# One of the conditioning's chunks is summed under ga and oa, and the first down projection makes a low part more in front of each four additions

## What is computed

```python
mod = (silu(c) @ ada_w + ada_b)          # ada_w is 1024 x 6144
shift_m, scale_m, gate_m, shift_f, scale_f, gate_f = split(mod, 6)
h = rmsnorm(x, pre_norm_mix) * (1 + scale_m) + shift_m
...                                       # h @ w_in, attention, state space mixer
x = x + gate_m * rmsnorm(mix, post_norm_mix)
h2 = rmsnorm(x, pre_norm_ffn) * (1 + scale_f) + shift_f
x = x + gate_f * rmsnorm(swiglu(h2), post_norm_ffn)
```

## Time and the profile before

| | us |
|---|---|
| median of 3 runs | 1008.52 (1007.31 to 1011.36) |
| the profiled execution's own time | 1003.94 |
| its span, from the first instruction to the last | 1002.2 |
| PE busy | 947.4 (95%) |
| DVE busy | 666.9 (67%) |
| ACT busy | 544.0 (54%) |
| POOL busy | 292.9 (29%) |

### The profile page before, as it was taken

One profiled execution on the slowest core, in us unless ns is written; L12 is line 12 of the kernel. 1 busy time (PEld: TensorE's weight loads), 2 busy tenths in 40 slices (PEclk: granted clock), 3 DMA queues, 4 the chain that ended last, 5 costly groups with the idle time before them and its releaser, 6 DMA issues.

```text
span 1002.2 us, 16492 instructions
## 1 busy us (share of the span) xinstructions
PE 947.4 (95%) x6119; PEld 831.1 (83%) x6119; DVE 666.9 (67%) x1067; ACT 544.0 (54%) x956; POOL 292.9 (29%) x260
## 2 busy tenths in 40 slices
PE   7999998999989989889999999989989989999997
PEld 6987777888877788789989999988879878888786
DVE  4765656777787568975567656677966577755553
ACT  5567565444433666834456456557863664444443
POOL 4304114111123455689951034330230241000010
PEclk9999999999999999999999999999999999999999
DMA  9755336789989713562028566652226667665562
GB/s 258 224 168 156 120 117 207 237 272 284 283 276 334 221 58 96 157 169 74 22 64 286 176 168 185 172 148 85 85 86 227 218 194 226 217 217 170 191 219 74
DMA packets 141467, 179.03 MB, mean 179 GB/s; under 512 B 8010, under 2 KB 117260, under 8 KB 141392
## 3 DMA queue, kind: packets, MB, share of 16 engines
q1 hardware_dynamic: 130624, 144.53, 46.4%
q0 software_dynamic: 10176, 33.16, 11.3%
q10 hardware_dynamic: 592, 0.34, 0.1%
HBM read 176.89 MB, written 1.12 MB: 178 GB/s over the span
## 4 chain that ended last, share of the span: by engine, by line
PE 80%; DVE 8%; ACT 5%; DMA 3%; issue 2%; POOL 1%; ACTq 0%; DVEq 0%; SPq 0%
PE bank L1923 26%; PE bank L2012 12%; PE bank L2014 12%; PE bank L2013 12%; DVE w_lo L1334 2%; ACT w_hi L873 1%; PE bank L2050 1%; PE bank L2181 1%; DVE isc L1727 1%; PE bank L1954 1%; PE bank L2460 1%; PE bank L2440 1%; PE bank L2436 1%; PE bank L2375 1%; PE bank L2547 1%
## 5 line engine op out<-in xcount | busy, mean ns | idle before, releaser
L1334 DVE TENSOR_TENSOR w_lo<-w_raw,w_hi 128x1024 fp32r<-128x1024 f32 (+1 forms) x227 | 274.7, 1236 | 94.3 <-ACT w_hi L873 88.0
L873 ACT ACTIVATE w_hi<-w_raw 128x1024 fp32r<-128x1024 f32 (+1 forms) x258 | 261.8, 1036 | 131.0 <-PE bank L2014 53.9
L1923 PE MATMUL bank<-h_hi,w_hi 128*128 128x256 f32 x560 | 163.4, 292 | 6.2 <-POOL w_lo L705 2.1
L1923 PE MATMUL bank<-h_lo,w_hi 128*128 128x256 f32 x560 | 158.3, 283 | 0.0
L1923 PE MATMUL bank<-h_hi,w_lo 128*128 128x256 f32 x560 | 158.2, 282 | 0.0
L2012 PE MATMUL bank<-w_hi,h_hi 128*128 128x512 f32 x384 | 152.3, 397 | 1.9 <-DVE h_lo L1334 1.9
L2014 PE MATMUL bank<-w_hi,h_lo 128*128 128x512 f32 x384 | 150.2, 391 | 0.0
L2013 PE MATMUL bank<-w_lo,h_hi 128*128 128x512 f32 x384 | 150.1, 391 | 0.0
L705 POOL TENSOR_TENSOR w_lo<-w_raw,w_hi 128x1024 fp32r<-128x1024 f32 (+1 forms) x39 | 86.4, 2215 | 149.6 <-DVE w_lo L1334 112.3
L1923 PEld LDWEIGHTS bank<-h_hi,w_hi 128*128 128x128 f32 x560 | 107.2, 191 | 7.8 <-POOL w_lo L705 2.3
L1923 PEld LDWEIGHTS bank<-h_lo,w_hi 128*128 128x128 f32 x560 | 107.3, 192 | 0.0
(11 more groups left out here) (458 smaller groups left out, 1850.8 us busy)
## 6 DMA issues: line engine op xcount, KB each, us to landing
w_raw<-in_w_in SPq DMA_DIRECT2D x84, 512.0 KB, 3.8
ada_raw<-in_ada_w POOLq DMA_DIRECT2D x48, 512.0 KB, 6.0
w_raw<-in_w_gate_up SPq DMA_DIRECT2D x88, 256.0 KB, 5.3
w_raw<-in_w_ffn_in SPq DMA_DIRECT2D x88, 256.0 KB, 3.8
w_raw<-in_w_down SPq DMA_DIRECT2D x22, 512.0 KB, 6.7
w_raw<-in_w_ffn_out SPq DMA_DIRECT2D x22, 512.0 KB, 4.4
w_raw<-in_w_out SPq DMA_DIRECT2D x16, 512.0 KB, 4.2
w_raw<-in_w_o_ssd SPq DMA_DIRECT2D x16, 512.0 KB, 3.5
```

The costliest lines, as they stand in the source:

```text
L873: act.activation(high(u, n), w_raw[:, u % RING, 0:n], ACT.Copy).then_inc(hi_ready, 1)
L1334: return dve.tensor_tensor(dst, src, hi.bitcast(F32), ALU.subtract)
L1923: ins = pe.matmul(out_b[:, s, :], w[:, kk, c], x[:, k0 + k, :], start=k == 0 and s == 0 and step == 0, stop=k == sum(st.ks) - 1 and s == 1 ...
```

## The change

`MOD_CHUNKS` gives the columns a new order: the chunk counters 0 to 6 stand for the chunks 0, 1, 2, 3, 6, 7 and 4 (shift_m, scale_m, shift_f and half of gate_m), the counters 7 to 9 for chunks 8, 9 and 5 (scale_f and the other half of gate_m). Counters 0 to 6 are summed up to the first down projection, counters 7 to 9 under ga and oa, three steps in each block instead of two. Under the first down projection there are four turns instead of six, and each `split_to` reaches one unit further, so that in the first turn one low part stands in front of the additions, and the pairs of the later turns end one unit further on.

`store_sums` and `finish_mod` follow the new order: the first store is three DMAs instead of two, the second two instead of one, the first load of `mod` two instead of one. The second `finish_mod` loads rows 0 to 39, works on all 48 rows, and stores rows 16 to 23 and 32 to 39. `mod` is set to zero once at the start.

```diff
@@ -519,6 +519,8 @@
     n_rows_dma = 9
+    MOD_CHUNKS = (0, 1, 2, 3, 6, 7, 4, 8, 9, 5, 10, 11)
+    MOD_FIRST, MOD_SECOND = 7, 10
@@ -729,36 +731,49 @@
             pool.dma_start(ada_raw[:, j, :].rearrange("p (k c) -> p k c", k=2),
-                           ada[:, 2 * j:2 * j + 2, 512 * c:512 * c + 512]).then_inc(ada_in[j], 16)
+                           ada[:, 2 * j:2 * j + 2, 512 * MOD_CHUNKS[c]:512 * MOD_CHUNKS[c] + 512]).then_inc(ada_in[j], 16)
         def store_sums(part):
             pool.wait_ge(sums_read, part + 1)
             if part == 0:
-                for g in range(2):
-                    pool.dma_start(sums_dram[2 * D * g:2 * D * (g + 1)].rearrange("(j n) -> j n", j=4),
-                                   sums[0:P:32, g, :]).then_inc(sums_out, 16)
+                pool.dma_start(sums_dram[0:2 * D].rearrange("(j n) -> j n", j=4), sums[0:P:32, 0, :]).then_inc(sums_out, 16)
+                pool.dma_start(sums_dram[3 * D:4 * D].rearrange("(j n) -> j n", j=2), sums[0:64:32, 1, :]
+                               ).then_inc(sums_out, 16)
+                pool.dma_start(sums_dram[2 * D:2 * D + 512].rearrange("(j n) -> j n", j=1), sums[64:65, 1, :]
+                               ).then_inc(sums_out, 16)
+            elif part == 1:
+                pool.dma_start(sums_dram[4 * D:5 * D].rearrange("(j n) -> j n", j=2), sums2[0:64:32, 0, :]
+                               ).then_inc(sums_out, 16)
+                pool.dma_start(sums_dram[2 * D + 512:3 * D].rearrange("(j n) -> j n", j=1), sums2[64:65, 0, :]
+                               ).then_inc(sums_out, 16)
...
-            pool.wait_ge(sums_out, (32, 48, 64)[part])
+            pool.wait_ge(sums_out, (48, 80, 96)[part])
+        mod_parts = (((0, 20), (24, 32)), ((0, 40),), ((32, 48),))
+        mod_stores = (((0, 32),), ((16, 24), (32, 40)), ((32, 48),))
         def finish_mod(n, r0, r1):
+            for a0, a1 in mod_parts[n]:
+                pool.dma_start(mod[a0:a1, :], sums_dram[P * a0:P * a1].rearrange("(r n) -> r n", n=P)).then_inc(sums_in, 16)
+            pool.wait_ge(sums_in, 16 * (5 + sum(len(p) for p in mod_parts[:n + 1])))
             at_rows = slice(r0, r1)
-            pool.dma_start(mod[at_rows, :], sums_dram[P * r0:P * r1].rearrange("(r n) -> r n", n=P)).then_inc(sums_in, 16)
-            pool.wait_ge(sums_in, 16 * (n + 6))
...
-            pool.dma_start(mod_dram[P * r0:P * r1].rearrange("(r n) -> r n", n=P), mod[at_rows, :]).then_inc(mod_out, 16)
-            pool.wait_ge(mod_out, 16 * (n + 1))
+            for a0, a1 in mod_stores[n]:
+                pool.dma_start(mod_dram[P * a0:P * a1].rearrange("(r n) -> r n", n=P), mod[a0:a1, :]).then_inc(mod_out, 16)
+            pool.wait_ge(mod_out, 16 * sum(len(p) for p in mod_stores[:n + 1]))
...
+        pool.memset(mod[:, :], 0.0)
         link(pool.memset(mod_g[:, :], 1.0))
@@ -771,10 +786,9 @@
-        for h in range(16):
-            if h < 14:
-                for j in (0, 1) if h % 2 == 0 else (2, 3):
-                    load_ada(h // 2 + 1, j)
+        for h in range(2 * (MOD_FIRST - 1)):
+            for j in (0, 1) if h % 2 == 0 else (2, 3):
+                load_ada(h // 2 + 1, j)
@@ -813,17 +827,16 @@
         pool.wait_ge(uv_mm, 4)
-        for j in range(4):
-            load_ada(8, j)
-        for j in range(4):
-            load_ada(9, j)
+        for c in range(MOD_FIRST, MOD_SECOND):
+            for j in range(4):
+                load_ada(c, j)
...
-        finish_mod(1, 32, 40)
+        finish_mod(1, 0, 48)
@@ -1256,7 +1269,7 @@
-        act.activation(sums2[0:64, 0, :], bank[6][0:64, :], ACT.Copy).then_inc(sums_read, 1)
+        act.activation(sums2[0:96, 0, :], bank[6][0:96, :], ACT.Copy).then_inc(sums_read, 1)
@@ -1656,8 +1669,8 @@
         gate_up(0, s_gu)
-        for h in range(6):
-            split_to(s_dn.u0 + AHEAD + 2 * h)
+        for h in range(2 * (MOD_FIRST - 5)):
+            split_to(s_dn.u0 + AHEAD + 2 * h + 1)
             modulate(5 + h // 2, 4 * (h % 2), 4 * (h % 2) + 4)
         boundary(1, 0)
@@ -1787,10 +1800,12 @@
         for b in range(s_ga.n):
             split_to(s_ga.u0 + 2 * b + 2 + AHEAD)
-            modulate(8, 2 * b, 2 * b + 2)
+            for step in range(3 * b, 3 * b + 3):
+                modulate(MOD_FIRST + step // KD, step % KD, step % KD + 1)
         for b in range(s_oa.n):
             split_to(s_oa.u0 + 2 * b + 2 + AHEAD)
-            modulate(9, 2 * b, 2 * b + 2)
+            for step in range(3 * (s_ga.n + b), 3 * (s_ga.n + b) + 3):
+                modulate(MOD_FIRST + step // KD, step % KD, step % KD + 1)
@@ -2357,7 +2372,7 @@
-                between={(0, 0): last, (1, 0): lambda: add_up(0, 8, 0), (1, 5): shift_transpose})
+                between={(0, 0): last, (1, 0): lambda: add_up(0, MOD_FIRST, 0), (1, 5): shift_transpose})
@@ -2482,7 +2497,7 @@
-        add_up(8, 10, 6)
+        add_up(MOD_FIRST, MOD_SECOND, 6)
```

More of the change, by code:

```diff
@@ L737, in store_sums @@
             if part == 0:
-                for g in range(2):
-                    pool.dma_start(sums_dram[2 * D * g:2 * D * (g + 1)].rearrange("(j n) -> j n", j=4),
-                                   sums[0:P:32, g, :]).then_inc(sums_out, 16)
-            else:
-                pool.dma_start(sums_dram[D * (3 + part):D * (4 + part)].rearrange("(j n) -> j n", j=2),
-                               (sums2 if part == 1 else sums)[0:64:32, 0, :]).then_inc(sums_out, 16)
-            pool.wait_ge(sums_out, (32, 48, 64)[part])
+                pool.dma_start(sums_dram[0:2 * D].rearrange("(j n) -> j n", j=4), sums[0:P:32, 0, :]).then_inc(sums_out, 16)
[8 more added lines that the diff above has]
+                               ).then_inc(sums_out, 16)
+            else:
+                pool.dma_start(sums_dram[5 * D:6 * D].rearrange("(j n) -> j n", j=2), sums[0:64:32, 0, :]
+                               ).then_inc(sums_out, 16)
+            pool.wait_ge(sums_out, (48, 80, 96)[part])
+        mod_parts = (((0, 20), (24, 32)), ((0, 40),), ((32, 48),))
+        mod_stores = (((0, 32),), ((16, 24), (32, 40)), ((32, 48),))
         def finish_mod(n, r0, r1):
+            for a0, a1 in mod_parts[n]:
+                pool.dma_start(mod[a0:a1, :], sums_dram[P * a0:P * a1].rearrange("(r n) -> r n", n=P)).then_inc(sums_in, 16)
+            pool.wait_ge(sums_in, 16 * (5 + sum(len(p) for p in mod_parts[:n + 1])))
             at_rows = slice(r0, r1)
-            pool.dma_start(mod[at_rows, :], sums_dram[P * r0:P * r1].rearrange("(r n) -> r n", n=P)).then_inc(sums_in, 16)
-            pool.wait_ge(sums_in, 16 * (n + 6))
             link(pool.tensor_tensor(mod[at_rows, :], mod[at_rows, :], mod_b[at_rows, :], ALU.add))
@@ L867, in split @@
             if s_lat.u0 <= u < s_lat.u0 + 4:
-                act.wait_ge(sums_out, 32)
+                act.wait_ge(sums_out, 48)
             elif u in held:
@@ L1281, in _ @@
         act.wait_ge(cum_ready, 1)
-        act.wait_ge(sums_out, 48)
+        act.wait_ge(sums_out, 80)
         for i in range(KI + 4):
```

## The result

| | before | after |
|---|---|---|
| median of 5 runs, us | 1008.52 (1006.44 to 1011.36) | 1001.87 (1000.19 to 1003.07) |
| ratio | | 0.9929 [0.9904, 0.9955] |
| the profiled execution's own time, us | 1003.94 | 1003.07 |
| its span, us | 1002.2 | 1001.4 |
| its mean granted clock of TensorE | 0.994 | 0.994 |

The median is 6.3 us under the forecast and 2.1 us under the range. The two profiled executions tell another story: they differ by 0.8 us of span (forecast: 0.3). So the first thing to settle is why the medians of the two kernels lie 6.7 us apart while their profiles hardly differ.

A forecast was written before the change was run, and what follows sets the result against it. TensorE, busy 95% of the span, was taken as the bound. The sum was 1002.2 - 1.4 (head) + 1.1 (handoff) = 1001.9 us of span, so the median goes from 1008.52 to 1008.2 us, range 1004.0 to 1012.3.

The forecast's parts named there:

- the last of the sum: From span to median: the profiled execution's 4.6 us under the median carries over, so the median goes from 1008.52 to 1008.2.
- The low part in front of the additions: Start of first down projection: unit 2 gains 2.8 us, unit 3 newly stalls about 1.4 us, net gain 1.4 us.
- faster landings or a freer DVE give nothing there: First down projection: removing eight additions and four 512 KB loads gains nothing, PE having no gap after 294.5.
- The lead holds at units 5, 7 and 9: First down projection: low parts of these units are ready in time, with margins of 0.2, 0.4 and 0.5 us.
- The head's term: Start of the first down projection: net gain of 1.4 us, bounded by 0 and 2.8.
- nobody waits for them: POOL's nine small loads behind `gu_T` start up to 10 us sooner, at no cost.
- rival 4: First down projection: the stall only moves on to unit 3 and units 5, 7, 9; head gain 0, median 1009.6; chance 0.14.
- The handoff: Sums and `mod` through DRAM before the transpose: extra store and load pieces add 1.1 us, all paid by PE.
- Rival 2: Handoff through DRAM: pieces serialize, plus 5.0 us instead of 1.1, median 1012.1; chance 0.09 with its half-way case.
- Rival 1: Handoff through DRAM: less traffic makes the chain 0.4 us shorter instead of 1.1 longer, median 1006.7; chance 0.14.
- Under ga and oa, the second store, the rest: Later blocks and POOL's later work: extra additions, loads and DMAs cost 0, with a DMA share of 0.92.
- Rival 3: Under ga and oa: DMA runs short, a weight unit lands late, plus 5.5 us, median 1013.7; chance 0.03.

The follow-up runs named there:

- five later comparisons: The changed kernel, no edit, timed again five times against the kernel before: ratios 0.9992, 0.9982, 0.9978, 0.9977 and 0.9971.
- the chunks alone: The changed kernel with the old `split_to`, so one chunk less is summed early but low parts stand as before: ratio 1.0017 against the kernel before.
- the pieces alone: The kernel before with its first store of sums in three DMAs and its first load of `mod` in two: ratio 0.9987.
- the low parts alone: The kernel before with each `split_to` under the first down projection reaching one unit further, all eight chunks kept there: ratio 1.0010.

## Why the prediction was wrong

**The step that failed is the last of the sum:** "The profiled execution lies 4.6 us under the median of the three runs shown; a difference carries over", with "a median of the new kernel may stand about 3 us to either side of its case". The 4.6 us are no fixed offset between a profiled execution and a median. They are the spread of single executions, and this spread goes with the granted clock. Against that kernel's mean of 1006.73 us at 0.9872, the median stood 1.8 us above and the profiled execution 2.8 us below; it had 0.994, for which the fit gives 0.0068 x 590 us = 4.0 us below. All five executions of the new kernel in the first comparison had 0.994 or 0.995, mean 0.9944, so its median came out near the profiled execution and not above it. The 6.65 us between the medians then go like this, by the fit: 0.6 us the program, 0.0072 x 590 = 4.2 us the clock of the five, and 1.8 us because the five of before (1008.52) stood above that kernel's usual 1006.73; together 6.6. The second term is measured. That the third is clock too is inferred from the slope, since those executions have no clock on record. My range had room for 3 us of such spread on one side; 6.3 came. The medians of the five later comparisons, 1004.3 to 1005.6 us, all lie in the range. The row with the 4.6 us should have warned me: where one execution stands 4.6 us from the median, a set of five can too, if they share a condition.

**Still open.** Why the chip grants one execution less than another. Why the first five all stood within 0.001 where other sets spread over 0.01: of the 60 later executions 12 had 0.994 or more, so five out of five would come about once in 3000 times if executions were independent; what they shared, no run shows. And whether the change itself raises the clock a little. Over the later comparisons it stands 0.0018 ± 0.0011 higher, worth 1.1 us. A candidate is the wait of 2.7 to 2.9 us before unit 2, which the change takes away and behind which the clock fell in one profile of four; the two variants that keep it, the chunks alone and the pieces alone, stood at 0.9853 and 0.9865. But the low parts alone, without it, stood at 0.9874, and 0.0018 would be about one fall less in each execution, and no run shows that.

**The mechanism, point by point.**

- *The low part in front of the additions:* right. Unit 2 at 291.74 (forecast 291.7), the stall moved to unit 3, 1.2 us from start to start for 1.4. With the nine small loads held back the head is 34.9 us, 1.4 us under the 36.3 of before, which is the forecast term. It is a gain only with the chunk taken away: alone it turns into 1.21 us before `add_up`, a point of the change that I had put at nothing ("faster landings or a freer DVE give nothing there").
- *The lead holds at units 5, 7 and 9:* wrong at 9 or 10. The head's term was -1.4 us; in six profiles of the changed kernel the head takes 36.0 us in the mean (35.6 to 36.3), in two of before 36.3, so the term is about -0.4. What failed is the price of the nine small loads, "nobody waits for them". Nobody waits for what they bring, but a weight unit waits for what they take: a wait at unit 9 or 10, of 0.34 to 1.05 us in all, stands in all six profiles of the changed kernel, and none in the kernels that only hold the nine loads back. So rival 4 (the stall only moves on) was partly right, though by a mechanism that I hadn't named in it.
- *The handoff:* mis-sized. +1.1 us less 0.24 was forecast; the six profiles of after give 35.7 us in the mean and two of before 35.5, and the pieces alone 35.8. That is 0.1 to 0.3 us. The pieces are issued 0.5 to 0.6 us apart as forecast, and POOL's arithmetic on `mod` begins 0.3 to 0.8 us later than in the two profiles of before, and 1.3 to 1.4 later with the pieces alone. But in 14 of the 17 profiles, both of before among them, the store of `mod` is issued 9.74 or 9.75 us behind the first store of the sums: the first arithmetic step takes the longer the sooner it starts (1.50 us from 5.85, 0.61 from 6.75) and ends at 7.35 us. The step that failed is "each microsecond of it is PE's": the chain had up to 0.9 us of slack in that step. What holds POOL there, no run shows. The wait at the transpose is 0.85 to 2.04 us over the six, the longest where another step took 1.54 us for 0.45. Rival 2, serial pieces, is out: two pieces more would cost 5.0 us, and cost under 0.5. The Trainium skill (DMA: Bandwidth & Descriptors, Anatomy of one DMA — SWDGE (gpsimd) path) gives about 2.0 us fixed for each DMA. The last piece of the sums, of 2 KB, landed here 1.60 us after its issue, 0.4 us under that, and the pieces overlap, so that a sum over them doesn't hold.
- *Rival 1, a shorter handoff:* the store of `mod` took 4.21 to 4.93 us in the six profiles, not 3.2 (4.71 and 4.38 before); out.
- *Under ga and oa, the second store, the rest:* right. No new wait, a share of 0.89 for 0.92, `add_up` six matmuls without a wait. Rival 3 is out.

The span's forecast, -0.3 us, stands against -0.6 ± 0.4 at the same clock and -0.8 in the first profiles. That the sum over the program came out is luck in part: the head's term was 1.0 us too good and the handoff's 0.7 us too bad.

## What to carry to other kernels

Read the mean granted clock beside every time, and compare times at the same clock before explaining a difference; where one profiled execution stands far from the median, take that distance as the spread of a median too. In a stage whose DMA share is near 1, count every transfer that a shortened loop lets start sooner, also those for which nobody waits. Where an engine only waits for a handoff, put its consumer as late as its reader allows: that was worth 1.8 us here, more than the change itself at the same clock.

## What the runs showed of the hardware

The clock fell to half for 3.4 us in the middle of matmuls without gaps, 1.4 us behind an idle of 2.05 us, and in another execution of the same kernel with the same idle it did not. Behind two waits of PE of 3.7 to 4.3 us it fell in all 17 profiles, behind those of 1.7 to 3.1 us in some. A kernel that keeps PE busy 95% of its span ran at mean clocks of 0.980 to 0.996, worth 0.59 us for each 0.001. Nine small loads, of 1 to 128 KB and 0.5 to 0.9 us apart, went with a longest landing of a 512 KB weight load of 10.7 and 13.2 us, against 8.6 and 8.9 with the nine held back, and made PE wait up to 1.5 us for a unit. A step of POOL's arithmetic on 32x128 elements took 0.56 to 1.50 us in 14 profiles, by when it began, and ended at the same point; its cause is open.
